# A decoder trunk on one core: the input projection by visits, the first modulation in quarters, partial sums added by GpSimd

## The reference

```
mod = silu(c) @ ada_w[layer] + ada_b[layer]          # 2048 x 12288 per layer
sh_m, sc_m, g_m, sh_f, sc_f, g_f = split(mod, 6)
h = rmsnorm(x, norm_mix) * (1 + sc_m) + sh_m
x = x + g_m * mixer(h)
h = rmsnorm(x, norm_ffn) * (1 + sc_f) + sh_f
x = x + g_f * ((silu(h @ w_gate) * (h @ w_up)) @ w_down)    # width 5632
```

## Time and profile before

| | |
|---|---|
| Time, median of 3 runs | 2389.53 us (2387.75 to 2392.1) |
| The profiled execution | 2390.23 us, span 2388.5 us |
| Busy, share of the span | PE 2256.0 (94%), DVE 1618.3 (68%), ACT 1055.7 (44%), POOL 103.2 (4%) |
| Chain that ended last | PE 91%, DVE 3%, DMA 3%, ACT 1%, issue 1% |
| DMA | 615.86 MB, mean 258 GB/s |

### The profile page before, as it was taken

How to read it: one execution, slowest core, us unless ns; L and a number is a source line. 1 busy time by engine, 2 the same in 40 slices (tenths; PEclk the granted TensorE clock), 3 DMA queues, 4 the chain that set the end, 5 groups by cost and what they waited for, 6 DMA issues and landing times.

```text
span 2388.5 us, 26350 instructions
## 1 busy us (share of the span) xinstructions
PE 2256.0 (94%) x10172; PEld 1865.8 (78%) x10172; DVE 1618.3 (68%) x1570; ACT 1055.7 (44%) x1330; POOL 103.2 (4%) x71
## 2 busy tenths in 40 slices
PE   0489999989999999999999999999999999999998
PEld 0368888778888888888887888887888888888886
DVE  6778887877766777666777777787674455454454
ACT  2244655364444334444446444446444433444443
POOL 0001210100000010000010000010000001000010
PEclk9989999999999999999999999999999999999999
DMA  8979878968888888888886888886886666666663
GB/s 318 336 283 356 303 276 295 314 229 299 277 271 283 277 279 292 281 270 284 275 286 223 274 276 274 274 286 207 308 273 181 190 193 193 192 189 188 190 192 124
DMA packets 269644, 615.86 MB, mean 258 GB/s; under 512 B 19792, under 2 KB 20176, under 8 KB 269136
## 3 DMA queue, kind: packets, MB, share of 16 engines
q1 hardware_dynamic: 268080, 613.50, 76.7%
q10 hardware_dynamic: 1440, 0.69, 0.1%
HBM read 612.02 MB, written 2.10 MB: 257 GB/s over the span
## 4 chain that ended last, share of the span: by engine, by line
PE 91%; DVE 3%; DMA 3%; ACT 1%; issue 1%; SPq 0%; DVEq 0%; ACTq 0%
PE ps L1024 29%; PE ps L1026 29%; PE ps L1025 29%; DMA ada<-ada_w 3%; PE ps L1075 2%; DVE acc L699 2%; PE ps L1054 1%; ACT hf L440 1%; PE ps L1063 1%; DVE wlo L673 0%; DMA raw<-w_out 0%; ACT whi L379 0%; DMA raw<-w_in 0%; PE ps L1187 0%; PE ps L1206 0%
## 5 line engine op out<-in xcount | busy, mean ns | idle before, releaser
L673 DVE TENSOR_TENSOR wlo<-raw,whi 128x1024 fp32r<-128x1024 f32 x776 | 959.6, 1240 | 655.8 <-ACT whi L379 655.3
L379 ACT ACTIVATE whi<-raw 128x1024 fp32r<-128x1024 f32 x776 | 823.5, 1062 | 1199.6 <-PE ps L1026 1119.6
L1024 PE MATMUL ps<-whi,h 128*128 128x512 f32 x2144 | 854.4, 399 | 34.6 <-DVE wlo L673 26.7
L1025 PE MATMUL ps<-wlo,h 128*128 128x512 f32 x2144 | 840.1, 392 | 0.0
L1026 PE MATMUL ps<-whi,h 128*128 128x512 f32 x2144 | 839.9, 392 | 0.0
L1024 PEld LDWEIGHTS ps<-whi,h 128*128 128x128 f32 x2144 | 406.0, 189 | 124.3 <-issue 26.8
L699 DVE SCALAR_TENSOR_TENSOR acc<-ada,cact,acc 128x1024 f32<-128x1024 f32 x368 | 483.7, 1314 | 26.7 <-DMA ada<-ada_w 18.7
L1025 PEld LDWEIGHTS ps<-wlo,h 128*128 128x128 f32 x2144 | 406.4, 190 | 85.7 <-issue 3.8
L1026 PEld LDWEIGHTS ps<-whi,h 128*128 128x128 f32 x2144 | 405.8, 189 | 85.8
L1024 PE MATMUL ps<-whi,act 128*128 128x512 f32 x704 | 274.7, 390 | 0.0
L1026 PE MATMUL ps<-whi,act 128*128 128x512 f32 x704 | 274.0, 389 | 0.0
(11 more groups left out here) (115 smaller groups left out, 808.3 us busy)
## 6 DMA issues: line engine op xcount, KB each, us to landing
ada<-ada_w SPq DMA_DIRECT2D x384, 512.0 KB, 5.4
raw<-ff_gate SPq DMA_DIRECT2D x176, 512.0 KB, 4.2
raw<-ff_up SPq DMA_DIRECT2D x176, 512.0 KB, 3.8
raw<-ff_down SPq DMA_DIRECT2D x176, 512.0 KB, 4.2
raw<-conv_in SPq DMA_DIRECT2D x96, 512.0 KB, 4.3
raw<-w_in SPq DMA_DIRECT2D x88, 512.0 KB, 6.3
raw<-w_out SPq DMA_DIRECT2D x32, 512.0 KB, 7.0
raw<-conv_out SPq DMA_DIRECT2D x32, 512.0 KB, 5.3
```

The costliest lines, as they stand in the source:

```text
L379: nc.scalar.activation(whi[v % SPLIT][:, :, :], raw[:, v % RAW], ACT.Copy).then_inc(hi_ready, 1)
L673: nc.vector.tensor_tensor(wlo[v % SPLIT][:, :, :], raw[:, v % RAW], whi[v % SPLIT][:, :, :].bitcast(F32), ALU.subtract).then_inc(lo_ready, 1)
L1024: nc.tensor.matmul(to, high, whi[v % SPLIT][:, k, :], start=begin, stop=False)
L1025: nc.tensor.matmul(to, high, wlo[v % SPLIT][:, k, :], start=False, stop=False)
```

## The change

**Visits.** Units of w_in are put in another order. A visit is one group of columns with some of the four row quarters k. First all 11 groups of columns are visited with quarter 0 of the features alone (units 0 to 10), then six groups (EARLY) three times with one quarter each (units 11 to 28), then the other five once with quarters 1 to 3 (units 29 to 43). A visit is evicted to SBUF: the first of a group of columns to `kept` or `vtok`, a later one to one of four slots `visit`, from which GpSimd adds it to what is kept (`add_visit`, two adds of 128 x 512, for 23 visits). Rope, gelu and the value product wait for the sum (`whole`).

**Quarters.** The first modulation goes by quarters of the features: 16 `acc` steps, each on 512 columns of shift beside 512 of scale, make a quarter. One quarter stands ahead of unit 0; the other three are made by unit 19, turned and scaled behind units 9, 15 and 21, and first used in units 11, 17 and 23. `ada_to` then gives 2.4 steps a unit up to 64, and 2.8 up to 160. The total up to unit 57 is 160, as before. Angles and sines of rope move behind units 3 and 5.

**Low pieces.** Of pieces 57, 61, 65 to 117, every fourth, 16 in all, the low part is made by GpSimd (POOL_LOW).

**Heads** move from units 19 to 39 to units 28 to 42, closer together, and w_out is taken in another order (OUT_UNITS). **Slots**: RAW 5 for 6, ADA_SLOTS 6 for 4, one `junk` for two.

```diff
-RAW = 6
+RAW = 5
-ADA_SLOTS = 4
+ADA_SLOTS = 6
-IN_COLS = (6, 7, 0, 3, 1, 4, 2, 5, 8, 9, 10)
-V_GROUPS = (0, 1, 8)
+IN_ORDER = (0, 3, 6, 1, 4, 7, 2, 5, 8, 10, 9)
+EARLY = 6
+VISITS = ([(c, (0,)) for c in IN_ORDER]
+          + [(c, (k,)) for k in (1, 2, 3) for c in IN_ORDER[:EARLY]]
+          + [(c, (1, 2, 3)) for c in IN_ORDER[EARLY:]])
...
+OUT_UNITS = ([(n, k) for ks in ((0, 1), (3, 2)) for n in range(2) for k in ks]
+             + [(n, k) for n in range(2, 4) for k in range(4)])
...
+POOL_LOW = tuple(range(57,118,4))
...
-ADA = ([(0, w, n) for n in range(2) for w in (SC_M, SH_M)]
+ADA = ([(0, SH_M, q) for q in range(4)]
        + [(0, w, n) for w in (G_M, SC_F, SH_F, G_F) for n in range(2)]
...
+ANGLES_AT, TRIG_AT = 3, 5
+REDUCE_AT = {8: 1, 14: 2, 20: 3}
...
 def ada_to(u):
 
+    if u < 0:
+        return KT
+    if u < 22:
+        return min(4 * KT, KT + (12 * (u + 1)) // 5)
     if u < U_F0 - 2:
-        return min(ADA_FIRST + 96, ADA_FIRST + (5 * (min(u, U_OUT + 5) + 1)) // 3 + 3 * max(0, u - U_OUT - 5))
-    return min(ADA_OPS, ADA_FIRST + 96 + u - (U_F0 - 3))
+        return min(10 * KT, 4 * KT + (14 * (u - 21)) // 5)
+    return min(len(OPS), 10 * KT + u - (U_F0 - 3))
...
+TURNS = [[(t, q) for q in range(4) for t in range(2)]] + 4 * [((0, 0), (0, 1), (1, 0), (1, 1), (0, 2), (1, 2), (0, 3), (1, 3))]
...
-SCORE_UNIT = (19, 21, 23, 25, 27, 29, 31, 33, 35, 37, 38, 39)
+SCORE_UNIT = (28, 29, 30, 33, 34, 35, 36, 37, 38, 39, 41, 42)
...
-        zq = at("zq", 44, [2, COLS])
-        zk = at("zk", 48, [2, COLS])
+        kept = at("kept", 0, [len(KEPT), 2, COLS])
+        visit = at("visit", 44, [4, COLS])
...
-        junk = sb("junk", [P, 2, COLS], mybir.dt.bfloat16)
+        junk = sb("junk", [P, COLS], mybir.dt.bfloat16)
...
+        def low_done(engine, v):
+
+            if v in POOL_LOW:
+                engine.wait_ge(pool_low, POOL_LOW.index(v) + 1)
+            else:
+                engine.wait_ge(lo_ready, v + 1 - sum(p < v for p in POOL_LOW))
...
+        def whole(engine, v, t):
+
+            engine.wait_ge(kept_added, 2 * ADDED.index(v) + t + 1)
...
             def load_piece(v):
                 if v >= RAW:
-                    sp.wait_ge(lo_ready, v - RAW + 1)
+                    low_done(sp, v - RAW)
...
+                if j < QUARTERS:
+                    to = to.rearrange("p (w n) -> p w n", w=2)
+                    src = w.rearrange("p (w n) -> p w n", w=6)[:, SH_M:SC_M + 1, COLS * n:COLS * n + COLS]
...
-            for a in range(ADA_SLOTS, ADA_FIRST):
+            for a in range(ADA_SLOTS, KT):
                 load_ada(a)
-                if a >= 36 and a % 4 == 0:
-                    load_piece((a - 36) // 4)
-            load_piece(7)
-            for u in range(2, U_END):
+            for v in range(4):
+                load_piece(v)
+            for u in range(U_END):
...
+            def add_visit(v):
+                i, c = ADDED.index(v), VISITS[v][0]
+                for t in range(2):
+                    freed(pool, v, t)
+                    if BEFORE[v] in ADDED:
+                        whole(pool, BEFORE[v], t)
+                    else:
+                        freed(pool, BEFORE[v], t)
+                    of = kept_of(c, t)
+                    nc.gpsimd.tensor_tensor(of, of, visit[:, (2 * i + t) % 4, :], ALU.add).then_inc(kept_added, 1)
+
+            for u in range(U_F0):
+                for v in (2 * u + 4, 2 * u + 5):
+                    if v in POOL_LOW:
+                        pool.wait_ge(hi_ready, v + 1)
+                        nc.gpsimd.tensor_tensor(wlo[v % SPLIT][:, :, :], raw[:, v % RAW],
+                                                whi[v % SPLIT][:, :, :].bitcast(F32), ALU.subtract).then_inc(pool_low, 1)
+                if VISIT_AT.get(u) in ADDED:
+                    add_visit(VISIT_AT[u])
+                for i in range(3):
+                    for kind in range(2):
+                        if UNIT_OF[LAST[(Q, K)[kind][i]]] == u:
+                            rope(i, kind)
+                for r, (g, n, t, on_ve) in enumerate(RES[:8]):
+                    if not on_ve and GROUP_END[g] == u:
+                        residual(r)
...
+            def keep_visit(v, t):
+
+                if v in ADDED:
+                    i = 2 * ADDED.index(v) + t
+                    if i >= 4:
+                        sa.wait_ge(kept_added, i - 3)
+                    evict(visit[:, i % 4, :], v, t)
+                else:
+                    evict(kept_of(VISITS[v][0], t), v, t)
...
+            for a in range(KT):
+                if a == 12:
+                    for t in range(2):
+                        mean(0, t)
+                    for t in range(2):
+                        inverse(0, t)
                 ada_op(a)
...
+            ve.wait_ge(const_loaded, 16 * N_CONST)
+            gain_quarter(0)
+            lo_piece(0)
+            norm_lo(0, 0)
+            lo_piece(1)
+            norm_lo(0, 1)
+            lo_piece(2)
+            lo_piece(3)
...
-            for n in range(2, 46):
+            for n in range(46):
...
+                if n == ANGLES_AT:
+                    angles()
+                if n in REDUCE_AT:
+                    gain_quarter(REDUCE_AT[n])
+                if n - 1 in REDUCE_AT:
+                    norm_lo(0, 2 * REDUCE_AT[n - 1])
+                    norm_lo(0, 2 * REDUCE_AT[n - 1] + 1)
...
+            norm_turn(0, 0)
+            norm_turn(0, 1)
             reduce_cols(0)
-            reduce_cols(1)
-            norm_units(0, U_IN, G_IN)
```

More of the change, by code:

```diff
@@ L273, in weight_pieces @@
         def weight_pieces():
[L275 to L280, removed]
+            for v, c, k in IN_UNITS:
+                for half in range(2):
+                    yield piece_of(w_in_v, 2 * k + half, c)
+            for n, k in OUT_UNITS:
+                for half in range(2):
+                    yield piece_of(w_out_v, 2 * k + half, n)
             yield from feed_pieces(0)
@@ L359, in _ @@
             pool.wait_ge(trig_ready, 4)
[L360 to L367, removed]
+            def add_visit(v):
[23 more added lines that the diff above has]
+                        residual(r)
+            for r in range(8, len(RES)):
+                if not RES[r][3]:
+                    residual(r)
         @block.scalar
@@ L385, in keep_row @@
             def keep_row(u):
[L386 to L388 removed]
+                for j, n in ADA_AT[u]:
+                    if is_row(j):
                         half = ADA[j][2]
[L390 removed]
+                        gate = GATES.index(ADA[j][:2])
                         if gate:
@@ L825, in feed, with head_lo, gain_quarter @@
                     u += nu + 4 * nd
-            ve.wait_ge(cact_ready, 1)
-            for a in range(KT):
-                ada_op(a)
-            for t in range(2):
-                mean(0, t)
-            for t in range(2):
-                inverse(0, t)
-            for a in range(KT, KT + 2):
-                ada_op(a)
-            ve.wait_ge(const_loaded, 16 * N_CONST)
-            keep_cols(0)
+            def head_lo(n):
+                m = SCORE_AT.get(n - 4)
+                if m is not None:
+                    ve.wait_ge(o_hi, m + 1)
+                    nc.vector.tensor_tensor(mixed[:, m, S:2 * S], ps[:, O_BANK, 0:S], mixed[:, m, 0:S].bitcast(F32),
+                                            ALU.subtract).then_inc(o_ready, 1)
+            def gain_quarter(q):
+                keep_cols(q)
+                col = mod_column(0, SC_M, 4 * q)
+                ve.wait_ge(mod_done, q + 1)
+                nc.vector.scalar_tensor_tensor(out=gsc[:, 4 * q:4 * q + 4], in0=mod[:, col:col + 4], scalar=1.0,
+                                               in1=gain[:, 0, 4 * q:4 * q + 4], op0=ALU.add, op1=ALU.mult)\
+                    .then_inc(gsc_ready, 1)
             def angle(n, ins):
@@ L1152, in feed, with out_unit, heads_out @@
                     u += nu + 4 * nd
+            def out_unit(n):
+                m, k = OUT_UNITS[n]
+                ks = [q for i, q in OUT_UNITS if i == m]
+                ready, value = None, HEADS
+                if m == 0:
+                    ready = sg_ready if k == 3 else o_ready
+                    value = 2 if k == 3 else 4 * k + 4
+                unit(U_OUT + n, G_OUT + m, ks.index(k), 4, mixed, ready, lambda t: value, 4 * k)
+            def heads_out(n):
+                m = SCORE_AT.get(n - 4)
+                if m is not None:
+                    pe.wait_ge(pt_copied, m + 1)
+                    if m:
+                        pe.wait_ge(o_ready, m)
+                    rows, cols = reduced_by(n - 1)
+                    if rows:
+                        pe.wait_ge(row_done, rows)
+                    pe.wait_ge(mod_done, QUARTERS + cols)
+                    whole(pe, LAST[V[m // 4]], 1)
+                    nc.tensor.matmul(ps[:, O_BANK, 0:S], vtok[:, 0, P * m:P * m + P], probT[:, m % 2, 0:S],
```

(3 more changed lines are left out.)

433 lines of the change are left out of this document (218 added, 215 removed).

## The result

The changed kernel takes 2395.57 us (median of 11 runs, 2394.95 to 2397.9) against 2389.53 (11 runs, 2385.51 to 2392.1): ratio 1.0028, 95% interval 1.0019 to 1.0037. I had forecast 8 us faster. The time lies in the range, the sign is wrong.

What follows compares the result with a forecast made beforehand. VectorE was to bound the kernel from unit 11: 450.4 us busy, 38.7 idle and 2 for a late piece put the second norm at 491 us against 498.8, so 2390.2 - 8 = 2382 us; range 2342 to 2407.

Steps and rivals of the forecast that it cites:

- The bound: Layer-0 mixer from unit 11: VectorE needs 7.4 us a unit, later 8 to 8.7, against TensorE's 5.7, so TensorE waits.
- An add costs VectorE 1.03 and 0.85 us, +45.5: Units 11 to 43: GpSimd's 46 adds of visits slow VectorE, 1.03 us for 36 adds and 0.85 for 10.
- A low piece costs 2.07, +14 net: The 16 low pieces on GpSimd: 33 us of slowed VectorE work against 19 us taken off it.
- Busy, 450.4 in all: VectorE's work up to the second norm: 392.1 - 1.2 - 19 + 45.5 + 33 = 450.4 us.
- The start: Prologue: the 16th acc step ends at 31.8 us, and TensorE's first matmul comes at 37.4 us instead of 86.25.
- VectorE's idle time, 38.7: Up to the second norm: VectorE's start, lower clock, second quarter, units 2 to 10, gaps and 6 us reserve, 38.7 us.
- Slots: 0 to +1: DMA buffers: RAW 5 for 6 stays hidden, 0 to +1 us; ada loads held in SyncE's queue cost 0.
- 1 (GpSimd costs little): GpSimd's adds (0.34 us) and low pieces (1.03) cost VectorE little: 2336, some 2306 with no cost; chance 0.18.
- 2 (heads): Heads at units 28 to 42: waits for scores stay while VectorE is the bound, 25 us later, 2407; chance 0.2.
- 4 (clock: TensorE's pauses lower its clock; every second one of 49 units cold would add 44 us, 2430; chance 0.03.
- Rival 3: The gain of the start is given back whole, work +58 and idle -58: 2389 to 2391; chance 0.14.
- The signs: From 120 to 490 us, wlo and acc means staying at 1.3, TensorE waiting for GpSimd's pieces, or growing score waits.

Runs made afterwards that it cites:

- e2: Changed kernel with each of the 46 GpSimd adds of visits cut to one column of 512, sums left out: 2356.40 us.
- e5: Changed kernel with the 46 adds of visits made by VectorE straight from PSUM, low pieces still on GpSimd: 2374.06 us.
- e12: Changed kernel with each of the 46 GpSimd adds of visits made twice in a row: 2431.33 us.
- e6: Changed kernel with both the adds of visits and all low pieces on VectorE: 2359.38 us.
- e8: Changed kernel with the first modulation's acc steps at 18/7 a unit for 12/5, so the quarters' sums come sooner: 2382.57 us.
- e9: e6 with the first modulation's acc steps at 18/7 a unit for 12/5, as in e8: 2347.34 us.
- e13: Changed kernel with the edits of e3 and e8 together, sums of the input projection left out: 2331.50 us.
- e3: Changed kernel with GpSimd's adds cut to one column (sums left out) and the low pieces on VectorE: 2343.29 us.
- e1: Changed kernel with the 16 low pieces back on VectorE: 2381.61 us.
- e4: Changed kernel with each add of visits replaced by a GpSimd memset of the same 128x512 tile, sums left out: 2353.77 us.

## Why the prediction was wrong

- **The bound.** "TensorE then waits for VectorE" from unit 11 on: right in the main. VectorE was 93% busy (TensorE 85%, for some 75 expected), and every experiment that took VectorE's time made the kernel faster.
- **An add costs VectorE 1.03 and 0.85 us, +45.5.** Right: 0.82 each by e2's time and 0.90 by its busy time, 1.0 by e5's, 0.74 to 0.83 when doubled (e12), so 34 to 46 us.
- **A low piece costs 2.07, +14 net.** Measured 14.6 (12.3 by busy time). Right.
- **Busy, 450.4 in all.** The sum counts the `wlo` that begins at the mark, 1.2 us; without it the forecast is 449.2 at a mark of 490. Measured 440.9, 8 less. The prices of adds and low pieces hold, so most of this lies in the rest of VectorE's work: e6, less its 31.3 us of adds, has 383 where the terms of the sum give 390. Why is open. This error hid part of the next ones, which is luck.
- **The start.** The first matmul came at 43.82 us, not 37.4. Two terms were too small. The last step ended at 36.7 us, not 31.8, and the transfer rate wasn't what held it: by 36 us 12.7 MB had come (353 GB/s), more than the 11.2 that I counted. VectorE waited 6.45 us for a piece until 22.03 us (its timeline above), and the ten steps that were left then ran back to back at its own pace, some 1.4 us each, with 0.7 us of the norm between them. And the reduction took 3.57 us, not 1.8: I read the x16 of the earlier trace rows as two reductions, when it was one, its eight matmuls recorded twice each.
- **VectorE's idle time, 38.7: the step that failed.** It was 64.7. Up to 60 us VectorE was idle for 26.5 us where I had 18.2, 8 too few for the start. From 60 to 142 us, with the second quarter in it, it was 5.7 for 5.5. In the two windows of the third and fourth quarter it was 18.8, where I had nothing; the rest, 13.7, is near the 15 of gaps and reserve. I wrote that "what VectorE wants from others is long there". That looked at one direction. TensorE's reduction of a quarter waits for a step that VectorE makes in its own order, in step 13 or 19, while TensorE would be there some 6 us sooner. The two units of lead that were to hide everything are used up by it, twice. e8, e9 against e6 and e13 against e3 give 14.6, 13.4 and 14.8 us for this, and 16.0, 12.1 and 10.8 by the marks. e8 alone turns the sign: 7.9 us faster than the kernel before. So does e1, but what e1 gives back was in the forecast's sum, and what e8 gives back was not. That this is the forecast's 8 is luck, since the start was too cheap and the work too dear by about 8 us each.
- **Slots: 0 to +1.** For RAW right. That ADA_SLOTS would have helped the kernel before by 14 us I didn't see; it isn't part of the sign, but of what the rest of the change costs.
- **Rivals.** 1 (GpSimd costs little) fell with e1, e2 and e12. 2 (heads) fell: 0.6 us of waits on scores. 4 (clock, whose sum should read 2426 and not 2430) didn't come as every second unit at the lower level, but the granted clock was 0.87 to 0.91 from 120 to 320 us, and the estimate of 7 us above says that the clock has a part in what the stops cost. Where the stops go, the mark moves by more than the waits on `acc` that go with them: 16.0 for 11.1 us (e8), 12.1 for 10.6 (e9 against e6), 10.8 for 5.4 (e13 against e3). No run parts the stop from the lower clock, so how these sums divide stays open. Rival 3 (gain and price cancel) was the nearest, and a little beyond it: a gain of 59 us at most (e13), less 51 for GpSimd (e3) and 15 for the stops, is 7 us slower. Those three come from one chain of runs and add up by construction.
- **The signs.** Those that were to show me wrong (means that stay at 1.3 us, TensorE waiting for GpSimd's pieces, more waits on scores) all stayed away, and the sign was wrong all the same: none of them looked at the quarters' sums.

The 46 adds cost only 18 us on VectorE (e5 is 18.4 above e4, which has none), though their own work is 46 x 0.68 = 31. The marks say where some of it is: from e4 to e5 VectorE's busy time rises by 23 us and its idle time falls by 3, from e3 to e6 by 25 and 9, so part of the adds fills time in which VectorE waited. Open are the 6 to 8 us by which the busy time rises too little; the memsets and one-column adds that stand in e4 and e3, or ScalarE's 46 copies, may be behind it, and no run has either alone.

## What to carry to other kernels

Work moved from VectorE to GpSimd isn't free when both read SBUF and VectorE is the bound: here a piece of 1.2 us on VectorE cost it 2.0 to 2.1 us when GpSimd made it, and the same add was cheaper on VectorE, straight from PSUM, than hidden on GpSimd. When the forecast is a small difference of large terms (58 of work, 67 of idle time), go through every wait in both directions: a lead of two units hides what the slow engine wants, not what others want from a place in its queue. Give each such place its own term and its own sign of being wrong. And test a new order against the old one with the new buffer sizes: here they alone were worth 14 us.

## What the runs showed of the hardware

GpSimd and VectorE, both with two SBUF inputs, take turns in these traces: behind a running VectorE operation GpSimd's add gets in, the next VectorE operation lasts 1.0 to 1.1 us longer beside an add of 512 columns (about 2 us for a low piece of 1024, by e1), and the one behind it takes its usual 1.2 to 1.3 us. GpSimd's low piece lasted 3.0 us there. A memset of 512 columns (0.54 us) left VectorE's `wlo` at 1.33 us in the mean, the same as beside adds of one column. The eight one-column matmuls of a reduction took 3.57 us at 142.42 us, at a granted clock of 0.50, and 1.84 us at 96.16 us, at 1.00. The first one, at 36.75 us, took 3.57 us too, though the row of that stretch reads 1.00.
